# Hybrid NSA/GLA decoder step on one core: norm weights multiplied on GpSimd, and the input stage in another order

## The reference

```
def rms_norm(x, g):
    xf = x.astype(F32)
    xf = xf * lax.rsqrt(jnp.mean(xf * xf, axis=-1, keepdims=True) + NORM_EPS)
    return xf.astype(x.dtype) * g
...
    h = rms_norm(x, g_norm)
    (q, kv, gate, z_a, q_g, k_g, v_g, a_low, z_b, merge) = jnp.split(h @ w_in, _split_offsets(), axis=-1)
```

## Time and profile before

| | us |
|---|---|
| median of 3 runs | 1428.12 |
| lowest and highest | 1426.86, 1428.6 |
| the profiled execution | 1428.52 |
| its span in the trace | 1426.6 |

### The profile page before, as it was taken

The page is one execution under the profiler, slowest core; times in us unless marked ns, Lnnn a source line. Parts: engine busy times, 40 slices in busy tenths (PEclk is TensorE's granted clock), DMA queues, the critical chain, the costliest instruction groups (busy, mean ns, idle before and its releaser), DMA issues.

```text
span 1426.6 us, 23467 instructions
## 1 busy us (share of the span) xinstructions
PE 1341.1 (94%) x9489; PEld 1178.9 (83%) x9489; DVE 604.9 (42%) x1287; ACT 650.9 (46%) x1108; POOL 144.5 (10%) x179
## 2 busy tenths in 40 slices
PE   4999999998999999999999999999878879899998
PEld 4999899998878888888888888887555668899876
DVE  5311145536523433344333323333488755553242
ACT  5212245432334557655675567555657542221121
POOL 2100011104101000000000000002800080000000
PEclk9999999999999999999999999999789989999999
DMA  7251452412222212211221122202644455444231
GB/s 196 60 169 29 136 123 89 135 41 60 61 56 56 61 44 62 72 58 59 61 76 56 46 61 71 61 26 85 221 156 162 175 187 161 149 136 118 81 129 64
DMA packets 141243, 137.19 MB, mean 96 GB/s; under 512 B 27088, under 2 KB 125728, under 8 KB 141072
## 3 DMA queue, kind: packets, MB, share of 16 engines
q1 hardware_dynamic: 138352, 127.27, 29.2%
q0 software_dynamic: 2784, 8.43, 2.1%
HBM read 97.82 MB, written 41.88 MB: 98 GB/s over the span
## 4 chain that ended last, share of the span: by engine, by line
PE 68%; DVE 3%; ACT 2%; issue 1%; DMA 1%; SPq 1%; POOL 0%; POOLq 0%; DVEq 0%; ACTq 0%
PE ps L217 39%; PE ps L2196 6%; PE ps L1116 5%; PE ps L1149 5%; PE ps L1130 4%; PE ps L1163 1%; PE ps L1597 1%; PE ps L2108 1%; DVE S L2302 1%; PE ps L2204 1%; PE ps L2112 1%; PE ps L1091 0%; PE ps L2088 0%; PE ps L2163 0%; PE ps L1773 0%
## 5 line engine op out<-in xcount | busy, mean ns | idle before, releaser
L217 PE MATMUL ps<-hH,wH 128*128 128x352 f32 (+1 forms) x1320 | 444.3, 337 | 6.6 <-DVE hL L520 3.3
L217 PE MATMUL ps<-hH,wL 128*128 128x352 f32 (+1 forms) x1320 | 426.7, 323 | 0.0
L217 PE MATMUL ps<-hL,wH 128*128 128x352 f32 (+1 forms) x1320 | 425.9, 323 | 0.0
L217 PEld LDWEIGHTS ps<-hH,wH 128*128 128x128 f32 (+1 forms) x1320 | 248.3, 188 | 49.6 <-issue 37.8
L217 PEld LDWEIGHTS ps<-hL,wH 128*128 128x128 f32 (+1 forms) x1320 | 249.3, 189 | 2.8 <-issue 1.9
L217 PEld LDWEIGHTS ps<-hH,wL 128*128 128x128 f32 (+1 forms) x1320 | 248.2, 188 | 0.9
L1291 DVE CUSTOM_DVE_ANT_0 sP<-ps,dist 128x128 f32<-128x128 f32 (+3 forms) x128 | 57.7, 489 | 234.4 <-PE ps L1116 234.4
L1354 ACT ACTIVATE pPT<-ps 128x512 f32<-128x512 f32 (+3 forms) x104 | 49.1, 473 | 196.8 <-PE ps L1130 196.5
L204 DVE TENSOR_TENSOR wL<-w_raw,wH 128x1024 fp32r<-128x1024 f32 (+1 forms) x55 | 66.9, 1216 | 135.3 <-ACT wH L196 135.3
L1291 DVE CUSTOM_DVE_ANT_0 sP<-ps,dist,stat 128x512 f32<-128x512 f32 (+3 forms) x64 | 39.1, 649 | 132.7 <-PE ps L1116 132.7
L1395 ACT ACTIVATE sP<-sP,stat 128x640 f32<-128x640 f32 (+7 forms) x128 | 93.2, 730 | 2.9 <-DVE stat L1291 2.3
(11 more groups left out here) (365 smaller groups left out, 2100.5 us busy)
## 6 DMA issues: line engine op xcount, KB each, us to landing
w_raw<-in_w_in SPq DMA_DIRECT2D x46, 512.0 KB, 3.9
p_spill<-stg SPq DMA_DIRECT2D x132, 176.0 KB, 1.8
zt<-p_spill SPq DMA_DIRECT2D x24, 528.0 KB, 4.9
gvT<-p_spill SPq DMA_DIRECT2D x8, 528.0 KB, 5.9
rq<-p_spill SPq DMA_DIRECT2D x8, 528.0 KB, 4.9
x_all<-in_x_prompt SPq DMA_DIRECT2D x8, 512.0 KB, 9.9
w_raw<-in_w_in SPq DMA_DIRECT2D x16, 256.0 KB, 3.7
S<-in_state_gla SPq DMA_DIRECT2D x4, 1024.0 KB, 5.7
```

Of the source, the lines that this page charges most:

```text
L217: mm = nc.tensor.matmul(ps[0:t.m, bank, 0:NF], w[:, c % 2, t.m * k:t.m * k + t.m], x[:, k, NF * n:NF * n + NF], start=(k == 0 and i == 0), ...
```

## The change

There are four parts.

1. `norm_groups` becomes 0; 1; 2; 3 and 4; 5 and 6; 7 and 8.
2. For row tiles 2 to 8 GpSimd multiplies x by `ngb` in place, one after another, each once the tile is squared (ACT must have read it first) and the one before is done. DVE then multiplies by the row factor alone, once GpSimd is through with the tile (`x_scaled`). Tiles 0 and 1 stay as they were.
3. GpSimd sets `ssq`, `ident` and `tri` before its seven small transfers. ACT takes a root of a dummy value first, so that its table is loaded before the first square.
4. ACT's and DVE's lists of the stage stand in another order. PE's is unchanged.

```
@@ gpsimd
+            pool.memset(ssq, 1.0).then_inc(sem("consts"), 1)
...
             pool.dma_start(ab_col, a["gla_alpha_b"].rearrange("o (k p) -> p (o k)", p=P),
...
-            pool.memset(ssq, 1.0).then_inc(sem("consts"), 1)
...
+            pool.wait_ge(sem("ng_loaded"), 16)
+            for t in range(2, TILES):
+                n = rows_of(t)
+                pool.wait_ge(sem("squares"), t + 1)
+                nc.gpsimd.tensor_tensor(x_all[0:n, t, :], x_all[0:n, t, :], ngb[0:n, :], ALU.mult)\
+                    .then_inc(sem("x_scaled"), 1)
+                pool.wait_ge(sem("x_scaled"), t - 1)
             pool.wait_ge(sem("idx_ready"), 1)
@@ vector, normed
+                    if t >= 2:
+                        dve.wait_ge(sem("x_scaled"), t - 1)
+                        nc.vector.tensor_scalar(x_all[0:n, t, :], x_all[0:n, t, :], rstd[0:n, t:t + 1], None, ALU.mult)\
+                            .then_inc(sem("xn_ready"), 1)
+                        continue
@@ scalar
             act.wait_ge(sem("consts"), 1)
+            nc.scalar.activation(rstd[:, TILES - 1:TILES], ssq[:, 0:1], ACT.Sqrt).then_inc(sem("table_ready"), 1)
+            act.wait_ge(sem("table_ready"), 1)
```

More of the change, by code:

```diff
@@ L362, in sp_units @@
                     .then_inc(sem(f"p_stored{u % NSTG}"), 16)
-        norm_groups = ((0, 1), (1, 3), (3, 5), (5, 7), (7, TILES))
+        norm_groups = ((0, 1), (1, 2), (2, 3), (3, 5), (5, 7), (7, TILES))
         def x_bank(t):
@@ L456, in _ @@
         def _(pool):
+            pool.memset(ssq, 1.0).then_inc(sem("consts"), 1)
+            for m in (ident, tri):
+                pool.memset(m[:, :], 0.0 if m is ident else 1.0).then_inc(sem("consts0"), 1)
+            pool.wait_ge(sem("consts0"), 2)
+            pool.affine_select(out=ident[:, :], in_=ident[:, :], compare_op=ALU.not_equal, fill=1.0,
+                               base=0, pattern=[[-1, P]], channel_multiplier=1).then_inc(sem("consts"), 1)
+            pool.affine_select(out=tri[:, :], in_=tri[:, :], compare_op=ALU.is_ge, fill=0.0,
+                               base=0, pattern=[[1, P]], channel_multiplier=-1).then_inc(sem("consts"), 1)
             pool.dma_start(ab_col, a["gla_alpha_b"].rearrange("o (k p) -> p (o k)", p=P),
@@ L528, in _ @@
             low_of_h(0)
+            variance(2)
+            normed(2)
+            low_of_h(1)
             ring.low(dve, 0)
-            low_of_h(1)
-            variance(2)
             low_of_h(2)
-            normed(2)
             variance(3)
+            normed(3)
             ring.low(dve, 1)
-            normed(3)
             low_of_h(3)
             variance(4)
+            normed(4)
             low_of_h(4)
-            normed(4)
+            variance(5)
+            normed(5)
             low_of_h(5)
@@ L599, in _ @@
             high_of_h(0)
+            squares(2)
+            root(2)
+            high_of_h(1)
             ring.high(act, 0)
-            high_of_h(1)
-            squares(2)
             high_of_h(2)
-            root(2)
             squares(3)
@@ L611, in _ @@
             high_of_h(4)
+            squares(5)
+            root(5)
             high_of_h(5)
```

## The result

The changed kernel is slower, by about half of what was forecast. Over 22 runs each the median is 1431.45 us against 1428.14; the ratio is 1.0021, with a 95% interval from 1.0011 to 1.0030. That is 3.0 us, 1.6 to 4.3 (the medians differ by 3.3). The forecast was 6.5.

What follows compares the result with a forecast made beforehand. PE's chain, 68% of the span, was taken as the bound, its input stage passing from engine to engine. Turn 7 6.5 us late made 1428.52 into 1435.0, or 1434.6 against the median, 0.4 lower; range 1429.2 to 1439.5.

Steps and rivals of the forecast that it cites:

- The mechanism of the product: Input stage: GpSimd's 2.36 us plus DVE's 0.7 lengthen square to normed tile from 1.3 to 3.1 us.
- The lead: PE's input stage: first product 2.1 us earlier, at 21.8; lead gone by tile 3's turn, at 27.4 against 27.57.
- the holding: Input stage: DVE's products with a column and two-SBUF-input instructions stand still while GpSimd multiplies; chance of this walk 0.57.
- the link: Input stage: GpSimd's product of 2.36 us as a step between a tile's square and DVE's product.
- Rival (a): Input stage: GpSimd and DVE don't hold each other; turn 7 1.8 us late, time 1429.9 us; chance 0.20.
- Rival (c): Input stage: DVE's product with a column costs 1.2 us and is held; time 1440.6 us; chance 0.10.
- Rival (b): Input stage: faster, the 2.1 us lead survives if tile 4 is normed by 25.5; time 1424.7 us; chance 0.07.
- Rival (d): Input stage: the walk's waits are short by about as much as it gains; time stays at 1428; chance 0.06.
- Nothing of the change touches this landing.: Input stage: tile 2's load still lands at 13.0 us, so most of turn 0's 3.7 us lead ends there.
- PE's pace: Input stage: after a 2 us gap PE stays slow; turn 5 and a half-product at slow pace last until 42.5.
- The rest of the kernel is shifted as a whole.: Behind turn 7: PE has no wait that bites, so turn 7's 6.5 us delay carries through to the end.
- the sign and its chance: Whole kernel: slower by more than 2.9 us, chance 0.67 plus 0.02; within it 0.24; faster by more 0.07.

Runs made afterwards that it cites:

- e2: e1 plus seven GpSimd products of the same sizes on a scratch area nobody reads; ratio to the kernel before 1.0054.
- e1: The changed kernel without its GpSimd product, DVE norming tiles 2 to 8 in one instruction again; ratio to the kernel before 0.9976.
- e6: e3 with the seven small transfers moved behind the square of tile 3; ratio to the kernel before 0.9972.
- e10: The kernel before, unchanged, traced once more; turn 7 started at 38.17 us against 39.31 in its first trace.
- e11: The changed kernel, unaltered, traced once more; turn 7 started at 42.95 us against 43.58 in its first trace.
- e7: e1 with the squares of tiles 5 and 6 ahead of tile 3's copy; ratio to the kernel before 0.9953.
- e8: e7 with the seven small transfers behind the square of tile 3; ratio to the kernel before 0.9961.
- e3: The kernel before with part 3 alone: constants ahead of the seven small transfers, dummy root first; ratio to the kernel before 0.9984.
- e5: The changed kernel with ACT's squares of tiles 3 to 8 ahead of the copies of tiles 2 to 4; ratio to the kernel before 1.0013.

## Why the prediction was wrong in size

**The mechanism of the product was right, step by step.** GpSimd's product took 2.37 us at the median (2.36 forecast), DVE's product with a column 0.75 alone (0.70), and it was held by GpSimd, the large form as the small one. That 0.70 came so near is in part luck: it rests on 16 ns between two rows of 32 columns, and their spread of 169 to 180 ns allowed 0.45 to 0.8. The lead shrank from 3.3 us at the first product to 1.8 at turn 3 (25.79 against 27.57) and was lost at turn 5, which waited 4.3 us (3.6 forecast). e2 shows the holding without the link. Rival (a), no holding, falls with e2 and with the rows at 23.31 and 32.92. Rival (c) falls with 0.75 us. Rival (b) fell as worked out: tile 4 wasn't normed by 25.5 (it was at 26.4). Rival (d), no change, falls with the interval and with e1.

**The step that failed: "Nothing of the change touches this landing."** The forecast took tile 2's landing at 13.0 us from the trace. With the constants ahead of the transfers it was squared at 11.58, and at 10.83 to 12.08 in the seven traces with constants first where a load is the last thing it waited for, against 12.17 to 13.07 in the three with transfers first. The part of the change that moved seven transfers back was costed at nothing because nobody needs them early. That they are in the way of what is needed was not asked. e6 shows it. They moved by 0.64 us only, not by the 1.3 forecast. Turn 2 started at 16.17 instead of 17.6, 1.4 us of the error.

How much this step is worth depends on the pair. In the first pair the square came 1.5 us earlier, in the second (e10 and e11) 0.35. The means of the two groups are 12.6 and 11.6 us, so about 1 us is put down to the change, and the rest of the 1.5 is that the forecast was made from a trace with a late landing.

**A smaller term, PE's pace.** Turn 6 was forecast 5.2 us after turn 5 and came 4.5 after it. PE's turn 5 ran at the slow pace (1.93 us) as forecast, but within the half-product behind it the matmuls fall from 0.49 us (at 38.30) to 0.33 (at 38.89), the fast pace. Here some 0.7 us were too many. The other steps were off by a few tenths each way. Together the stage was over-forecast by 2.2 us: 6.5 against 4.3. In the second pair pace is the larger term. The forecast said that PE "stays at the slow pace" in turns 3 and 4, 3.9 us; in the first trace they took 3.3 and in e11 1.97. Of the 1.7 us between 6.5 and 4.8 there, 0.35 is the landing and most of the rest is pace.

**From the stage to the time.** The remaining 1.3 us lie between the stage's 4.3 (4.8 in the other pair) and the 3.0 by time. The forecast said "The rest of the kernel is shifted as a whole." PE's instructions are the same in all these traces, so the same matmul can be compared. In the first pair the changed kernel is 4.2 us behind at 209 us, 3.4 from 600 to 1000, 2.4 at 1100 and 0.4 ahead at the end, in the stretch where the clock varies. In the second pair it is 4.8 behind at 100 us, 5.8 at 209, 5.4 from 600 to 1000 and 5.3 at the end, so nothing of the shift is given back there. The other kernels' times follow their turn 7 within 1 us, but for e7 and e8. The interval of the changed kernel's time reaches to 4.3, so the runs don't show that any of the shift is given back later, nor that it isn't. This stays open. So does how the 6 to 7 us of the product in the new order divide into link and holding: e2 shows that holding alone can cost 9.9 with the longer instruction, but no kernel had the link without the holding.

**Range.** Its lower end, 1429.2, lay under the measured median of 1431.45; the sign and its chance were right. What was too narrow was the trust in one landing time, and in one course of PE's pace, from one execution.

## What to carry to other kernels

Before work is moved to an idle GpSimd, look at which DVE instructions of the stage are products with a column or have two inputs in SBUF: they stand still while it multiplies, and e2's products cost 9.9 us without anybody waiting for them. Small early transfers are not free because their data is needed late; ask what lands behind them (e3 and e6: 1.4 to 2.5 us and then 1.4 more). When a change has several parts, run each alone: here one part was worth -1.4 to -2.5 us and another +5.9 to +6.9, and the sum looked like a small loss. And take a second trace of the kernel before a number is built on one landing: the two of the kernel before differ by 0.9 us there.

## What the runs showed of the hardware

- Holding depends on the form of the DVE instruction. Held while GpSimd multiplied: a product with a column of 128x1024 and of 128x2, and instructions with two SBUF inputs (the norm in e2, the weight tile's low part in e5). Not held: reciprocals of 128x2 (0.17 us) and the subtraction with an input in PSUM (1.21). That both sizes of the product with a column are held was assumed from 128x8; they are. ACT's squares and copies kept their 1.0 to 1.1 us, and so did DVE's norm (1.28 us) beside GpSimd's fill of 128x2048 in e2.
- GpSimd is held in turn, for less: its seven products took 2.34 to 2.71 us each in the changed kernel, and up to 3.24 in e2.
- Seven transfers of 1 to 16 KB, started on GpSimd's queue, delay 512 KB loads on SP's queue: tile 2's load took 6.9 to 7.0 us with them out of the way, 8.6 to 9.9 with them from 2.00 us on and 10.0 to 10.8 with them from 1.36 us on.
- While GpSimd starts those transfers (17.13 to 22.77 us in e6) DVE's variance of two columns takes 0.35 and 0.38 us instead of 0.17; the norm of two tensors keeps its 2.48 us.
- Two executions of the changed kernel differ between 1000 and 1240 us, at a granted clock of 0.91 and 0.88, by 4.4 us of span: as much as this change is worth.
